# Prompt recurrence of a hybrid decoder layer: three kinds of loads waited for apart, four steps put elsewhere in their queues, and level products over 64 moving columns instead of 128

## The reference

```
b = jnp.cumsum(gc, axis=2)                                   # gc = log f, k = 1 - f
inter = jnp.einsum('bhtd,bhdv->bhtv', qc * jnp.exp(b), S)
diff = b[:, :, :, None, :] - b[:, :, None, :, :]
decay = jnp.exp(jnp.where(mask[:, :, None], diff, -jnp.inf))
A = jnp.einsum('bhtd,bhtsd,bhsd->bhts', qc, decay, kc)
o = inter + jnp.einsum('bhts,bhsv->bhtv', A, vc)
S = jnp.exp(bl[:, :, 0])[..., None] * S + jnp.einsum('bhsd,bhsv->bhdv', kc * jnp.exp(bl - b), vc)
```

## Time and profile before

| | |
|---|---|
| median of 3 runs | 4056.15 us (4055.79 to 4062.39) |
| the profiled execution | 4059.26 us, its span 4057.5 us |
| busy over the span | PE 88%, PEld 70%, DVE 69%, ACT 55%, POOL 26% |
| the stage that is changed | about 678.6 to 930 us of the span |
| busy in it from 688 to 925 us | PE 178.3, PEld 162.8, DVE 166.0, ACT 162.9, POOL 144.4 us of 237 |

### The profile page before, as it was taken

One profiled execution on the slowest core, in us unless ns is written; L12 is line 12 of the kernel. 1 busy time (PEld: TensorE's weight loads), 2 busy tenths in 40 slices (PEclk: granted clock), 3 DMA queues, 4 the chain that ended last, 5 costly groups with the idle time before them and its releaser, 6 DMA issues. The chain is left out here.

```text
span 4057.5 us, 52643 instructions
## 1 busy us (share of the span) xinstructions
PE 3578.7 (88%) x18026; PEld 2857.0 (70%) x18027; DVE 2781.3 (69%) x4745; ACT 2218.7 (55%) x3701; POOL 1043.4 (26%) x1120
## 2 busy tenths in 40 slices
PE   8999998778877489885599998989999998999998
PEld 7878786677655235444388886868887887888886
DVE  6676665677788789888778885665556554555565
ACT  3343323676678589887667774335455444443232
POOL 0000002564311011100256730115556551000011
PEclk9999998999877689996699998989999999999999
DMA  6555444334200134434456633567667656554464
GB/s 169 171 144 162 139 124 134 108 111 143 76 23 25 52 145 167 156 115 128 113 196 214 233 133 120 198 207 224 200 208 234 201 178 204 183 182 150 134 217 139
DMA packets 387885, 624.83 MB, mean 154 GB/s; under 512 B 97560, under 2 KB 216440, under 8 KB 379320
## 3 DMA queue, kind: packets, MB, share of 16 engines
q1 hardware_dynamic: 309848, 312.05, 25.8%
q0 software_dynamic: 77376, 309.63, 22.8%
q10 hardware_dynamic: 416, 0.02, 0.0%
HBM read 444.81 MB, written 176.77 MB: 153 GB/s over the span
## 5 line engine op out<-in xcount | busy, mean ns | idle before, releaser
L3783 PE MATMUL up_acc<-x_parts_first,w_up_parts 128*128 128x512 f32 x1536 | 361.5, 395 | 14.1 <-DVE w_up_parts L3533 14.1
L738 PE MATMUL accumulated<-hT,w_in_parts 128*128 128x512 f32 x1536 | 359.1, 393 | 2.1 <-DVE w_in_parts L480 2.1
L3783 PEld LDWEIGHTS up_acc<-x_parts_first,w_up_parts 128*128 128x128 f32 x1536 | 293.1, 191 | 76.8 <-DVE w_up_parts L3533 15.3
L738 PEld LDWEIGHTS accumulated<-hT,w_in_parts 128*128 128x128 f32 x1536 | 289.0, 189 | 64.6 <-DVE w_in_parts L480 3.8
L2769 DVE TENSOR_SCALAR_CACHE_REDUCE junk_dve<-score,candidate 128x2048 bf16<-128x2048 f32 (+6 forms) x224 | 328.4, 1505 | 8.5 <-DVE candidate L2755 7.7
L3874 PE MATMUL down_acc<-w_down_parts_even,hidden_parts 128*128 128x512 f32 x1344 | 315.7, 392 | 12.5 <-DVE hidden_parts L3569 10.1
L3874 PE MATMUL down_acc<-w_down_parts_odd,hidden_parts 128*128 128x512 f32 x1344 | 312.7, 390 | 0.0
L3874 PEld LDWEIGHTS down_acc<-w_down_parts_even,hidden_parts 128*128 128x128 f32 x1344 | 254.0, 190 | 66.9 <-issue 14.0
L2692 ACT ACTIVATE junk_act<-score,candidate 128x1920 bf16<-128x1920 f32 (+6 forms) x224 | 286.4, 1294 | 24.7 <-DVEq L2756 15.9
L3874 PEld LDWEIGHTS down_acc<-w_down_parts_odd,hidden_parts 128*128 128x128 f32 x1344 | 251.8, 188 | 53.2 <-issue 1.0
L3335 ACT ACTIVATE hidden_parts<-hidden_raw 128x1024 fp32r<-128x1024 f32 x112 | 118.6, 1059 | 311.2 <-PE down_acc L3874 289.8
(11 more groups left out here) (541 smaller groups left out, 8665.6 us busy)
## 6 DMA issues: line engine op xcount, KB each, us to landing
hidden_raw<-scratch_hs POOLq DMA_DIRECT2D x112, 512.0 KB, 4.5
w_in_raw<-in_w_in SPq DMA_DIRECT2D x80, 512.0 KB, 4.1
up_raw<-scratch_ws SPq DMA_DIRECT2D x128, 256.0 KB, 3.0
scratch_hs<-hidden_even POOLq DMA_DIRECT2D x112, 256.0 KB, 4.9
scratch_hs<-hidden_odd POOLq DMA_DIRECT2D x112, 256.0 KB, 4.9
up_raw<-in_w_up SPq DMA_DIRECT2D x96, 256.0 KB, 5.6
weight_sums<-in_w_down POOLq DMA_DIRECT2D x16, 1024.0 KB, 5.2
scratch_wt<-weight_sums POOLq DMA_DIRECT2D x16, 1024.0 KB, 6.2
```

The costliest lines, as they stand in the source:

```text
L738: mm = pe.matmul(z, w2[:, g % 2, b, k2 * ST + n * P:k2 * ST + (n + 1) * P], h[:, a, k, :], start=(first and j == 0), stop=(last and j == 2))
L3783: mm = pe.matmul(up_bank(n), wp[:, n % SLOTS, b, q * P:(q + 1) * P], X(i)[:, a, q, :], start=(q == 0 and (a, b) == (0, 0)), stop=(q == QUA ...
```

## The change

It does five things, all in `recurrence_prompt`. (1) `in_rdy` becomes three semaphores, `k_in`, `b_in` and `qv_in`; each engine waits for those it uses. Loads go out as k, b, then q and v, each as soon as its own buffer is free, and the constants are waited for only where they are used. (2) SP issues chunk 0's loads before the constants, and the 36 loads for the next stage in two parts behind the loads of chunks 2 and 3. (3) `log_k` of the next chunk moves on ACT from behind n = 4 to behind n = 2; `middle` and `less_log_k` move on DVE to behind n = 4, ahead of the last two levels; POOL may subtract for n = 1 and 2 of the next chunk as soon as their buffer is free. (4) PE transposes `k_decayed` after slot 3 instead of after slot 5. (5) In slots 1 to 5 only the later halves of each pair are moving columns, so each product has 64 columns, packed; `pick` reads them packed.

```diff
-                    pool.wait_ge(in_rdy[par], 64 * j + 64)
+                    pool.wait_ge(b_in[par], 16 * j + 16)
...
-                        pool.wait_ge(exp_done, LEVELS * g + (n - 1 if n >= 3 else 0))
+                        if not (isinstance(g, int) and g == 0 and n < 3):
+                            pool.wait_ge(exp_done, LEVELS * g + n - (1 if n >= 3 else 2))
...
                             decayed(3).then_inc(kd_rdy, 1)
+                            if not is_last(g):
+                                log_k(g + 1, j + par, 1 - par)
                         if n == 3 and not first:
                             squares(g - 1, 1 - par)
-                        if n == 4 and not is_last(g):
-                            log_k(g + 1, j + par, 1 - par)
...
-                            _, of, _ = halves(level, l)
+                            of, mask = (a.rearrange("p (n m) -> p n m", m=1 << l) for a in (level[:, 0:RH * P // 2], second[:, slot - 1, :]))
...
-                        if n == 5 and not is_last(g):
+                        if n == 4 and not is_last(g):
                             middle(g + 1, j + par, 1 - par)
+                            less_log_k(g + 1, 1 - par)
...
-                            mm = pe.matmul(o[:, h * P:(h + 1) * P], x, x, start=True, stop=True)
+                            _, later, _ = halves(x, ORDER[slot + 1])
+                            mm = pe.matmul(o[:, h * P // 2:(h + 1) * P // 2], x, later, start=True, stop=True)
...
+                def next_inputs(g, par, before=None):
+                    sp.wait_ge(lv_done, SLOTS * g + 1)
+                    sp.sem_inc(spare, 1)
+                    load_k(g + 2, par)
+                    sp.wait_ge(exp_done, LEVELS * g + LEVELS)
+                    sp.sem_inc(spare, 1)
+                    load_b(g + 2, par)
+                    if before:
+                        store(g - 1, 1 - par)
+                        load_gate(g + 1, 1 - par)
+                    sp.wait_ge(s_done, g + 1)
+                    sp.sem_inc(spare, 1)
+                    load_qv(g + 2, par)
+                next_inputs(0, 0)
+                index_inputs(0)
+                next_inputs(1, 1, True)
+                index_inputs(1)
```

More of the change, by code:

```diff
@@ L816, in recurrence_prompt @@
         pT, pO, pS = ps("kd_T", [P, RH * P]), ps("o", [P, 2, RH * P]), ps("s_new", [P, RH * P])
-        const_rdy = sem("r_const")
-        in_rdy = [sem(f"r_in{b}") for b in range(2)]
+        const_rdy, ident_rdy = sem("r_const"), sem("r_ident")
+        k_in, b_in, qv_in = ([sem(f"r_{n}_in{b}") for b in range(2)] for n in ("k", "b", "qv"))
         gate_rdy = [sem(f"r_gate{b}") for b in range(2)]
@@ L858, in _, with turned, load_k, load_b @@
             def _(sp):
[L859 to L866, removed]
+                def turned(dst, src, g, par, done):
+                    sp.dma_start(dst[:, par, :, :], sc[src][:, :, bass.ds(g * P, P)].rearrange("h p t -> p h t")).then_inc(done[par], 16)
+                def load_k(g, par):
+                    turned(kt, "rkT", g, par, k_in)
+                def load_b(g, par):
+                    turned(bt, "rbT", g, par, b_in)
+                def load_qv(g, par):
+                    turned(qt, "rqT", g, par, qv_in)
                     sp.dma_start(vt[:, par, :, :].rearrange("p h v -> p (h v)"),
-                                 sc["ri"][bass.ds(g * P, P), :]).then_inc(in_rdy[par], 16)
+                                 sc["ri"][bass.ds(g * P, P), :]).then_inc(qv_in[par], 16)
                 def load_gate(g, par):
@@ L878, in store, with index_inputs @@
                                  mx[:, par, :, :].rearrange("p h v -> p (h v)")).then_inc(mix_out[par], 16)
[L879 to L887, removed]
+                load_k(0, 0)
+                load_b(0, 0)
+                load_qv(0, 0)
+                sp.dma_start(joined[:, :, :], io["levels_joined"]).then_inc(const_rdy, 16)
+                sp.dma_start(second[:, :, :], io["levels_second"]).then_inc(const_rdy, 16)
+                sp.dma_start(ident[:, :], io["ident"]).then_inc(ident_rdy, 16)
+                load_k(1, 1)
+                load_b(1, 1)
+                load_qv(1, 1)
+                load_gate(0, 0)
+                load_gate(1, 1)
+                def index_inputs(r2):
+                    if r2 == 0:
+                        for dst, n in (("identX", "ident"), ("same_query", "same_query"), ("unseen", "unseen_new")):
+                            sp.dma_start(ahead[dst].ap(), io[n]).then_inc(x_ld, 16)
+                        sp.wait_ge(x_zero, 2)
+                        sp.dma_start(kn[64:128, :, :], sc["kiT"][64:128, T:TA].rearrange("p (j t) -> p j t", j=NS)).then_inc(x_ld, 16)
+                    wsrc = sc["wi"][T:TA, :].rearrange("(j q) h -> h q j", q=TS)
                     for h in range(IH):
@@ L893, in _ @@
                         sp.dma_start(wd[r:r + TS, :], wsrc[h], allow_slow_non_contiguous=True).then_inc(x_ld, 16)
-                sp.wait_ge(x_ld, 16 * LOADS)
-                with sp.Fori(0, NCH // 2 - 1) as j:
-                    for par in range(2):
[L897 to L901, removed]
+                def next_inputs(g, par, before=None):
[15 more added lines that the diff above has]
+                index_inputs(1)
+                with sp.Fori(1, NCH // 2 - 1) as j:
+                    for par in range(2):
+                        next_inputs(2 * j + par, par, True)
+                store(NCH - 3, 1)
+                load_gate(NCH - 1, 1)
                 for par in range(2):
                     store(NCH - 2 + par, par)
+                sp.wait_ge(x_ld, 16 * LOADS)
                 for b in range(2):
@@ L958, in log_k @@
                 def log_k(g, j, par):
-                    act.wait_ge(in_rdy[par], 64 * j + 64)
+                    act.wait_ge(k_in[par], 16 * j + 16)
                     act.wait_ge(bk_rdy, g)
@@ L967, in decayed @@
                         return act.activation(kd[:, h, :], bk[:, par, h, :], ACT.Exp, bias=bt[:, par, h, P - 1:P], scale=-1.0)
-                    act.wait_ge(in_rdy[par], 64 * j + 64)
+                    act.wait_ge(b_in[par], 16 * j + 16)
                     if not (isinstance(g, int) and g < 2):
@@ L1023, in _ @@
                 dve.wait_ge(x_idx, 12)
-                dve.wait_ge(const_rdy, 48)
                 dve.sem_inc(mix_out[1], 16)
@@ L1063, in middle @@
                 def middle(g, j, par):
-                    dve.wait_ge(in_rdy[par], 64 * j + 64)
+                    dve.wait_ge(b_in[par], 16 * j + 16)
                     dve.tensor_scalar(mid[:, par, :], bt[:, par, :, P // 2 - 1], -1.0, None, ALU.mult).then_inc(spare, 1)
@@ L1083, in pick @@
                         if slot == 0:
+                            if first:
+                                dve.wait_ge(const_rdy, 32)
                             dve.copy_predicated(AT[:, par, :, :], joined[:, :, :].to_broadcast([P, RH, P]),
@@ L1088, in pick @@
                             _, out, _ = halves(flat(AT[:, par, :, :]), l)
-                            _, of, _ = halves(level, l)
-                            dve.copy_predicated(out, second[:, slot - 1, :].rearrange("p (n m) -> p n m", m=1 << l), of).then_inc(cp_done, 1)
+                            of, mask = (a.rearrange("p (n m) -> p n m", m=1 << l) for a in (level[:, 0:RH * P // 2], second[:, slot - 1, :]))
+                            dve.copy_predicated(out, mask, of).then_inc(cp_done, 1)
                     dve.wait_ge(eb_done, g + 1)
-                    dve.wait_ge(in_rdy[par], 64 * j + 64)
+                    dve.wait_ge(qv_in[par], 32 * j + 32)
                     if not (isinstance(g, int) and g < 2):
@@ L1107, in body @@
                             mean(g - 1)
-                        if n == 5 and not is_last(g):
+                        if n == 4 and not is_last(g):
                             middle(g + 1, j + par, 1 - par)
+                            less_log_k(g + 1, 1 - par)
                     if not first:
                         root_one(g - 1)
-                    if not is_last(g):
-                        less_log_k(g + 1, 1 - par)
-                    if not first:
                         root_two(g - 1)
@@ L1129, in _ @@
             def _(pe):
-                pe.wait_ge(const_rdy, 48)
                 def body(g, j, par):
-                    pe.wait_ge(in_rdy[par], 64 * j + 64)
+                    pe.wait_ge(k_in[par], 16 * j + 16)
+                    pe.wait_ge(qv_in[par], 32 * j + 32)
                     def bank_free(slot):
@@ L1156, in body @@
                             x = X[:, ORDER[slot + 1], h * P:(h + 1) * P]
-                            mm = pe.matmul(o[:, h * P:(h + 1) * P], x, x, start=True, stop=True)
+                            _, later, _ = halves(x, ORDER[slot + 1])
+                            mm = pe.matmul(o[:, h * P // 2:(h + 1) * P // 2], x, later, start=True, stop=True)
                         mm.then_inc(lv_done, 1)
```

(8 more changed lines are left out.)

## The result

The changed kernel takes 4087.82 us (4085.60 to 4089.55, 4 runs), the kernel before on the same footing 4057.45 us: a ratio of 1.0073 (95% interval 1.0057 to 1.0089). It is 30 us slower, where 4025 us and a gain were forecast.

The account below looks back on a forecast made before the run. A loop of waits, not a full engine, was taken to bound the kernel at 13.96 us a chunk. Start 6 us and chunks 25.5 us make 31.5 us saved from 4056.15: 4025 us, range 4010 to 4042.

Parts of the forecast that it names:

- Half the columns: 64 instead of 128 moving columns in slots 1 to 5: counted at nothing, bounds 0 and 0.5 us a chunk.
- a rival at 0.03: PE sits at 1.2 GHz through the stage: 102 us more than forecast, 4127 us; chance 0.03.
- About 58 us of low clock: Low clock in the stage that decides the sign, as 4.6 low chunks eat the 31.5 us saved.
- The rival's 6.8 us in 19.4: Excess of one chunk at 1.2 GHz, 19.4 us on PE's queue against the forecast chunk of 12.6.
- The steady chunk: Chunks take 12.6 us against 13.96; all 15 intervals 189.0 us, plus 4, against 218.47: 25.5 us saved.
- the walk: Path through DVE and PE: 5.07 us from last pick to slot 0's pick, then 7.5 to the last pick.
- the pacing by DVE and PE: Claim that, with ACT's loop at 11.3 us, a loop of DVE and PE sets the chunk at 12.6 us.
- Start: Stage start, chunk 0's loads ahead of the constants: 6 us saved, at least 3.6, at most 8.
- Chunk 2: Chunk 2's loads pass the 36 for the next stage: the long interval's extra 9.3 us goes, 4 given back.
- The give-back: k loads behind next-stage loads: about 3 us lost for chunk 3, 1 for chunk 4; together 4, between 0 and 6.
- POOL against DVE: Rival: DVE's multiplications and picks stretch beside POOL, about 1.1 us a chunk, chunk 13.7 us, total 4041 us; chance 0.15.
- The sign set for it: Forecast counts as wrong if DVE's multiplications have a mean above 0.65 us.

Follow-up runs that it names:

- e1: The changed kernel with 128 moving columns again in slots 1 to 5 and the pick as before: 4041.97 us, ratio 0.9956.
- e2: The kernel before with only the halved moving columns: 4107.63 us, ratio 1.0113.
- e5: The changed kernel, halved columns kept, plus one product a slot whose result nobody reads: 4045.55 us, ratio 0.9969.
- e9: e7 with the moved steps of ACT, DVE, PE and POOL undone: 4035.24 us, ratio 0.9941.
- e3: The kernel before with only the moved steps, loads and columns as before: 4124.14 us, ratio 1.0159.
- e6: e1 with POOL's four gathers for the next stage moved behind the last chunk's subtractions: 4036.65 us, ratio 0.9936.
- e7: e6 with the 36 loads for the next stage moved behind the loop: 4030.27 us, ratio 0.9927.
- e8: e7 with 26 products of zeros on PE before chunk 0: 4028.43 us, ratio 0.9925.

## Why the prediction was wrong

The profile says it by the prediction's own steps.

- **Half the columns, "I count this at nothing".** On PE's pace this was right: 0.97 us for eight loads with 64 moving columns as with 128. The sum's error is that the term was closed there: it measured 46 us, and with the other sign. It had a second way to act, through the clock, which stood in the text as a rival at 0.03. e1, e2 and e5 show it three ways: taken out of the changed kernel it gives back 46 us, put alone into the kernel before it costs 49 us, and covered by filler work it gives back 42 us.
- **The rival's reason against, "work per us goes up, not down, when the chunk is shorter",** is the sentence that failed. It counted chunks and not what PE does in them. The trace of before had the warning: chunk 8 dipped to 0.88 in the earlier trace rows, at full columns. A margin that thin should have carried a good share of the chance, with the edit that takes moving columns away from 20 products a chunk. The rival's price, 4127 us, assumed 1.2 GHz throughout; the clock was low about half the time in steady chunks, in each of these over the output and `s_new` products, and the price of that was 2.7 us a chunk (15.61 against e1's 12.87, both over the last eleven intervals). "About 58 us of low clock" was a slip beside it: 4.6 chunks of 19.4 us are 89 us. By the mean clocks the stage had some 150 us of low clock, and 33 in e1, for 46 us of time: 0.39 us for each of the 117 us between them. The rival's 6.8 us in 19.4 are 0.35.
- **The steady chunk, 12.6 us:** 12.87 in e1, where the clock stayed at 1.00. From slot 0's pick to the last the changed kernel needs 839.97 to 847.56, 7.6 us, for the 7.5 of the walk. The walk was right there, and so was the pacing by DVE and PE: e1's two waits of DVE for PE are 1.0 us a chunk, ACT's for `kd_T` 0.3.
- **What the walk paid for was put down to the wrong edit.** Of the 1.1 us from 13.96 to 12.87 most comes from the loads: without any moved step the chunk is 13.2 us (e9), and `log_k`, which waited 1.1 us a chunk for the DMAs before, shows no such wait in e9's steady chunks. The moved steps give 0.3 us. And they are a gain only together with the loads: alone they cost 65 us (e3), a rival that was missing.
- **Start, 6 us:** the first `q_exp_b` came 6.8 us after the stage's start and not 10.9, 4.1 us saved, and 4.0 in e1. `log_k` was done at 681.8, but `b_less_log_k` began only at 683.55, 5.7 us after the start instead of "about 4": DVE was still making the gathers' indices until 683.3. And what would be late next was not named: POOL's gathers. Chunk 0 grew by 5.6 us in e1 (19.3 against 13.7), so the saving was given back whole until e6.
- **Chunk 2, 9.3 us less 4:** the 23.3 us went, and ACT waited 4.5 us for chunk 3's k, in an interval of 16.4. The give-back was right in its place and, at 3.4 us over the 13.0 of e7, in its size (3 us forecast there).
- **POOL against DVE:** seen in part. The multiplications' mean is 0.655 us with the moved steps (e7) and 0.546 without (e9). Some of it falls where DVE would wait for PE anyway, so the chunk was 0.3 us over the forecast and not 1.1 as in the rival; that this stretching is also why the orders give so little is argued from the rows and was not tried by itself. The sign set for it, a mean above 0.65 us, was just passed in e1 and e7 (0.654 and 0.655), and not in the changed kernel (0.639).

Without the halved columns the change saves 17 us of the forecast 31.5 (e1); with gathers and index loads moved too, it saves 29 us (e7, against 4059.05 us on the same chip). e7 beats both kernels.

How TensorE's clock is decided stays open here. The runs show that fewer moving columns lower it and that filler work restores it; whether idle time weighs as much as columns was not separated. In e3, with full columns and long waits of PE (70.2 us for DVE's factors from 700 to 960 us), the stage's clock also fell, to 0.79.

## What to carry to other kernels

An edit that takes useless work off TensorE gains only if that work set the pace; look first whether the weight loads do. Then look at the granted clock around it: where it dips already, less work can cost more than it frees, and the products that pay may be others than those that were cut. When a wait is shortened, list what it had covered on every queue, here four gathers on POOL, and when a consumer moves up, check that its producer's signal comes as early.

## What the runs showed that was not expected

Twenty products a chunk with half the moving columns, at the same eight-load pace of 0.97 us at the full clock, brought the mean granted clock of the stage from 0.92 to 0.68 (e2). A filler of one product a slot brought it from 0.76 to 1.00 in the steady chunks and made the kernel 42 us faster. PE's busy share doesn't tell the two apart: 150.9 us of 171.8 at 0.76, 134.2 of 146.1 with fillers, and 116.1 of 141.2 in e1, also at 1.00. The Trainium skill (TensorE: Matmul & The Clock Gate, HAM oscillation) tells of the clock falling when TensorE waits for DMAs; here it fell in the changed kernel although PE waited less, 11.8 us for DVE's factors in chunks 3 to 13 against 29.0 us before, when its products got narrower. Low clock where little waits for PE cost nothing that shows: 0.80 against 1.00 over the first 20 us changed no interval by more than 0.1 us (e7, e8).
